# Opening a retention and convolution trunk layer pair by pair of channel tiles, with conditioning weights taken between the pairs

## The reference

```python
mod = silu(cond) @ ada_w + ada_b           # (…, 6*1024): sh1, sc1, g1, sh2, sc2, g2
sh1, sc1, g1, sh2, sc2, g2 = jnp.split(mod, 6, axis=-1)
h = rms_norm(x, n1_pre) * (1 + sc1) + sh1
proj = h @ w_in                            # q, k, v, g, u_a, u_b, two gates
```

## Time and profile before

| | us |
|---|---|
| median of 3 runs | 2121.06 (2118.7 to 2122.29) |
| the profiled execution | 2119.73 |
| its span | 2117.9 |

### The profile page before, as it was taken

How to read it: one execution, slowest core, us unless ns; L and a number is a source line. 1 busy time by engine, 2 the same in 40 slices (tenths; PEclk the granted TensorE clock), 3 DMA queues, 4 the chain that set the end, 5 groups by cost and what they waited for, 6 DMA issues and landing times.

```text
span 2117.9 us, 30759 instructions
## 1 busy us (share of the span) xinstructions
PE 2075.9 (98%) x12055; PEld 1876.0 (89%) x12055; DVE 1647.5 (78%) x1946; ACT 828.2 (39%) x1378; POOL 832.8 (39%) x557
## 2 busy tenths in 40 slices
PE   7999999999999999999999999999999999999998
PEld 3888887887887999999999998899999999978886
DVE  3599699699699587787536536699989989878867
ACT  3512212212212366565548323353433334344344
POOL 1414315315316366665381220006666565570000
PEclk9999999999999999999999999999999999999999
DMA  9343432432432455545464444312223223258453
GB/s 308 122 133 101 138 115 101 138 117 99 136 105 96 166 162 168 181 143 158 166 221 152 130 167 147 110 32 77 79 63 94 63 70 87 83 197 290 139 179 115
DMA packets 233760, 283.08 MB, mean 134 GB/s; under 512 B 11441, under 2 KB 176145, under 8 KB 233617
## 3 DMA queue, kind: packets, MB, share of 16 engines
q1 hardware_dynamic: 180785, 212.41, 31.7%
q10 hardware_dynamic: 51424, 63.98, 8.9%
q0 software_dynamic: 1408, 4.72, 0.6%
HBM read 214.06 MB, written 67.01 MB: 133 GB/s over the span
## 4 chain that ended last, share of the span: by engine, by line
PE 86%; DVE 5%; POOL 2%; ACT 2%; SPq 2%; DMA 1%; issue 1%; ACTq 0%; DVEq 0%; POOLq 0%
PE ps L1130 85%; DVE f_cv L2937 1%; PE ps L1345 1%; POOL Wa_lo L2288 1%; SPq L766 1%; DMA x_all<-in_x_sample 1%; DVE T_lo L2918 1%; DMA r_raw<-rT_d 0%; DVE T_raw L2892 0%; PE ps L1393 0%; PE ps L1480 0%; POOL ada_l L2288 0%; DMA W_raw<-in_w_in 0%; PE ps L1184 0%; DVE Al L2976 0%
## 5 line engine op out<-in xcount | busy, mean ns | idle before, releaser
L2590 DVE SCALAR_TENSOR_TENSOR conv_y<-u_in,VC,conv_y 128x1167 f32<-128x1167 f32 x240 | 409.1, 1704 | 11.1 <-ACT conv_y L1759 4.7
L1130 PE MATMUL ps<-A_hi,Wa_hi 128*128 128x384 f32 x768 | 261.1, 340 | 0.5 <-DVE A_lo L2538 0.5
L1130 PE MATMUL ps<-A_hi,Wa_lo 128*128 128x384 f32 x768 | 258.3, 336 | 0.0
L1130 PE MATMUL ps<-A_lo,Wa_hi 128*128 128x384 f32 x768 | 258.3, 336 | 0.0
L2438 POOL TENSOR_TENSOR O_lo<-E,O_hi 128x512 fp32r<-128x512 f32 x78 | 124.4, 1595 | 290.5 <-ACT O_hi L1637 290.5
L2937 DVE SCALAR_TENSOR_TENSOR f_cv<-f_in,VF,f_cv 128x1023 f32<-128x1023 f32 (+1 forms) x176 | 209.8, 1243 | 2.4 <-ACT f_cv L2105 0.6
L2288 POOL TENSOR_TENSOR Wa_lo<-W_raw,Wa_hi 128x1024 fp32r<-128x1024 f32 x51 | 133.6, 2627 | 195.6 <-ACT Wa_hi L1637 195.4
L2288 POOL TENSOR_TENSOR ada_l<-ada_w,ada_h 128x1024 fp32r<-128x1024 f32 x32 | 90.7, 2834 | 240.2 <-ACT ada_h L1637 240.1
L1130 PE MATMUL ps<-Wb_hi,A_lo 128*128 128x512 f32 x432 | 169.3, 392 | 0.0
L1130 PE MATMUL ps<-Wb_hi,A_hi 128*128 128x512 f32 x432 | 169.1, 391 | 0.0
L1130 PE MATMUL ps<-Wb_lo,A_hi 128*128 128x512 f32 x432 | 168.8, 391 | 0.0
(11 more groups left out here) (342 smaller groups left out, 5467.2 us busy)
## 6 DMA issues: line engine op xcount, KB each, us to landing
F_raw<-in_ffn_w_up SPq DMA_DIRECT2D x44, 512.0 KB, 6.1
qt<-qkvg_d SPq DMA_DIRECT2D x36, 512.0 KB, 3.6
W_raw<-in_w_in SPq DMA_DIRECT2D x32, 512.0 KB, 5.3
W_raw<-in_w_in SPq DMA_DIRECT2D x64, 256.0 KB, 3.3
ada_w<-in_ada_w ACTq DMA_DIRECT2D x30, 512.0 KB, 4.5
F_raw<-in_ffn_w_down SPq DMA_DIRECT2D x30, 512.0 KB, 4.8
A_raw<-g_d SPq DMA_DIRECT2D x25, 512.0 KB, 4.2
g_d<-f_cv SPq DMA_DIRECT2D x22, 576.0 KB, 3.6
```

The costliest lines, as they stand in the source:

```text
L1130: return pe.matmul(out, l, r, start=start, stop=stop)
L2590: dve.scalar_tensor_tensor(out=y, in0=x, scalar=tap, in1=y, op0=ALU.mult, op1=ALU.add).then_inc(q.conv_step, 1)
```

## The change

The opening is reordered, and nothing of what is computed changes. The eight pieces of `ada_w` become four **pairs**: pair `p` is the scale piece and the shift piece of channel tiles 2p and 2p+1. Each pair has its own product, row copy, turn and `hscale`. The steps are in the order `STEPS`: channel tiles 0 to 3 of group 0, then of group 1 (pairs 0 and 1), tiles 4 and 5 of both groups (pair 2), 6 and 7 of both (pair 3), and then all eight of the third group. `first_u` does both products of a step one after the other; the products of pairs 1 to 3 stand behind steps 1, 3 and 7, their turns behind 1, 4 and 8.

Banks are short, since six are filled by both products from the start: one bank (`MOD_BANK`) holds conditioning, and one (`TURN_BANK`) all turned blocks, so `x_turn(j)` waits until ACT has read the block before (`hT_f`). `modulated` writes into one of three SBUF buffers (`h_buf`) instead of PSUM, `halves` reads them there, and ACT no longer writes `A_hi`. The twelve parameter rows are issued by ACT, the exponentials of the decay tables stand behind the first weight splits, and the masks in DVE's step 4.

The diff, cut to its core:

```diff
-        TURN_BANK = (5, 7, 6)
-        ON_ACT = lambda j: j < 2 * KT and j % KT % 3 == 1
+        TURN_BANK, MOD_BANK, ROW_BANK = 6, 7, 3
+        STEPS = ([(g, k) for g in (0, 1) for k in range(4)] + [(g, k) for p in (2, 3) for g in (0, 1) for k in (2 * p, 2 * p + 1)]
+                 + [(2, k) for k in range(KT)])
+        PAIR_FROM = (0, 2, 8, 12)
+        ADA_BEHIND = {1: 1, 3: 2, 7: 3}
+        ADA_TURN_BEHIND = {4: 2, 8: 3}
+        h_buf = [sq_t[:, 1, 0:TG], sq_t[:, 1, TG:2 * TG], rows[:, 0:3, :].rearrange("p r n -> p (r n)")]
...
             chunk_load(0)
-            ada_chunk(7)
+            chunk_load(1)
+            ada_pair(0)
+            ada_pair(1)
             x_load(1)
-            chunk_load(1)
+            ada_pair(2)
+            ada_pair(3)
...
             def x_turn(j):
-                g, k = divmod(j, KT)
-                if j >= 3:
-                    pe.wait_ge(q.hT_lo, j - 2)
+                g, k = step_of(j)
+                if j:
+                    pe.wait_ge(q.hT_f, j)
+                pe.wait_ge(q.xn_ok, 3 * g + 3)
...
+            ada_early(0)
+            row_turns()
+            ada_turn(0)
...
+                for j in range(N_A):
+                    while turned < min(j + 3, 3 if j < 2 else 4 if j < 4 else 16 if j < 16 else N_A):
+                        x_turn(turned)
+                        turned += 1
+                    if j < N_A - 2:
+                        for e in range(2):
+                            product(e, j)
+                    if j in ADA_BEHIND:
+                        ada_early(ADA_BEHIND[j])
+                        if j == 1:
+                            ada_turn(1)
+                    if j in ADA_TURN_BEHIND:
+                        ada_turn(ADA_TURN_BEHIND[j])
+                for e in range(2):
+                    for j in (N_A - 2, N_A - 1):
+                        last = product(e, j)
+                    last.then_inc(q.u_ps, 1)
...
             squares(0)
             split_w(0)
-            squares(1)
-            act.wait_ge(q.mod_ok, 2)
+            split_w(1)
+            decay_exp()
             for j in range(N_A):
+                if j in PAIR_FROM:
+                    act.wait_ge(q.mod_ok, PAIR_FROM.index(j) + 1)
                 modulated(j)
-                if j == 7:
-                    squares(2)
-                if j in (3, 15, 19, 21, 23):
-                    split_w((3, 15, 19, 21, 23).index(j) + 1)
+                if j == 3:
+                    squares(1)
+                if 12 <= j < 15:
+                    square(j - 6)
+                if j == 15:
+                    root(2)
+                if j in (17, 19, 21, 23):
+                    split_w((17, 19, 21, 23).index(j) + 2)
...
             for j in range(N_A):
+                if j in (0, 2):
+                    ada_rows_out(j // 2)
+                if j in PAIR_FROM:
+                    mods(PAIR_FROM.index(j))
+                if j == 4:
+                    decay_masks()
+                if j in (4, 16):
+                    meaned(1 if j == 4 else 2)
+                    normed(1 if j == 4 else 2)
                 halves(j)
+                if j in ADA_TURN_BEHIND:
+                    ada_rows_out(ADA_TURN_BEHIND[j])
```

More of the change, by code:

```diff
@@ new lines, in _, with product @@
+            ada_early(0)
+            row_turns()
+            ada_turn(0)
+            def first_u():
+                turned = 0
+                pe.wait_ge(q.vec_ok, 6)
+                def product(e, j):
+                    g, k = step_of(j)
+                    tiles = slice(3 * g, 3 * g + 3)
+                    o = ps[:, 3 * e + g, 0:TG].rearrange("p (t n) -> p t n", n=P)
+                    wh, wl = (x[chunk_slot(e)].rearrange("p (k n) -> p k n", k=KT) for x in (w_hi, w_lo))
+                    pe.wait_ge(q.hT_lo, j + 1)
+                    mm(o, wh[:, k, :], A_hi[:, tiles, k, :], k == 0, False)
+                    mm(o, wh[:, k, :], A_lo[:, tiles, k, :], False, False)
+                    return mm(o, wl[:, k, :], A_hi[:, tiles, k, :], False, k == KT - 1)
+                for j in range(N_A):
[4 more added lines that the diff above has]
+                        for e in range(2):
+                            if j == 0:
+                                pe.wait_ge(q.w_lo, e + 1)
+                            product(e, j)
[9 more added lines that the diff above has]
+                    last.then_inc(q.u_ps, 1)
@@ L1409, in _ @@
                 if s == -5:
[L1410 removed]
+                    pe.wait_ge(q.mod_ok, 6)
                     pe.transpose(ps[0:64, 6, 0:P], gm1[:, :], ident[:, :]).then_inc(q.gain, 1)
@@ L2561, in _, with ada_rows_out, mods @@
-            for j in range(N_A):
-                if j == 3:
-                    normed(1)
-                if j == 8:
-                    meaned(2)
-                    normed(2)
+            decay_tables()
+            def ada_rows_out(p):
+                dve.wait_ge(q.vecT, ada_summed(p))
+                dve.tensor_copy(ada_row(p), ps[0:2, MOD_BANK, :].rearrange("c (v n) -> c v n", v=2)).then_inc(q.vec_ok, 1)
+            def mods(p):
+                dve.wait_ge(q.ada_used, 4 * (p + 1))
+                dve.wait_ge(q.vec_ok, 2)
+                two = slice(2 * p, 2 * p + 2)
+                for v in (SH1, SC1):
+                    r = v * KT + 2 * p
+                    c = 4 * v
+                    ins = dve.tensor_tensor(mod[:, r:r + 2, :], ps[:, MOD_BANK, c:c + 4].rearrange("p (k c) -> p k c", c=2),
+                                            col2(V_ADAB + r, 2), ALU.add)
+                then(ins)
+                dve.scalar_tensor_tensor(out=hscale[:, two, :], in0=mod[:, SC1 * KT + 2 * p:SC1 * KT + 2 * p + 2, :], scalar=1.0,
+                                         in1=col2(V_N1PRE + 2 * p, 2), op0=ALU.add, op1=ALU.mult).then_inc(q.mod_ok, 1)
```

225 lines of the change are left out of this document (89 added, 136 removed).

## The result

The changed kernel takes **2147.78 us** (median of 4 runs, 2145.52 to 2149.06), the kernel before 2121.07 on the same chip: a ratio of **1.0123, 95% interval 1.0112 to 1.0135**, 26.7 us slower. The forecast was 2143, range 2134 to 2152.

The account below looks back on a forecast made before the run. PE was taken as the bound: 85.4 of work + 14.4 waits + 5.0 port + 1.7 clock end `first_u` at 106.5. The later start made 2117.9 + 22 a span of 2140, median 2143 us, range 2134 to 2152.

Parts of the forecast that it names:

- Start: Opening: pair 0's product from 16.6 for 8.9 us, then an unhidden chain; first `first_u` product at 33.4 instead of 47.95.
- The central argument: After the first product: conditioning only moved on in-order PE; 52.0 us remain, ending at 85.4, so at best 1.5 us won.
- Waits and port: In `first_u`: PE's waits made by the pairs, 14.4 us, plus DVE's sums held by POOL's splits, 5.0.
- hand-over of pair 1: Behind pair 1's product: row copy, `hscale`, `modulated(2)`, turn and halves make PE wait 3.5 us.
- The port: Last steps of `first_u`: DVE's two-SBUF-input sums wait for POOL's split subtractions, 5.0 us (bounds 0 and 9.6).
- chain to `ada_l`: Behind the last halves: transfers, splits and `ada_l` up to the product, 22.2 us as before; what follows starts 22.7 later.
- Clock: Opening: only the hole before the first product drops PE's clock, twelve products mostly at 0.32; 1.7 us, bounds 0 and 6.
- a wait of 2 to 3 us for `ada_l`: Sign in the new trace: PE waits this long for `ada_l` in the fourth tile of `q_half(0)`.
- The waits close: Rival for `first_u`: halves and turns keep ahead, clock stays up, PE ends at 85.4; 2119 to 2123 us, chance 0.06.
- half of them close: Rival for `first_u`: port costs nothing, clock stays, DVE's SBUF instructions are quicker; loss 4.2 to 13 us, chance 0.08.
- More half clock: Rival for the opening: each hole lowers the clock and the last group runs at 0.32; 2153 to 2165 us, chance 0.06.
- It comes back later: Rival for everything after the opening: later slack gives the loss back; no share of its own.

Follow-up runs that it names:

- after_short: The changed kernel with only one of eight matmuls in each conditioning product of pairs 1 to 3; 2134.90 us, ratio 1.0067 to the kernel before.
- fill: The changed kernel plus 92 idle transposes on PE in places where it waits; 2146.63 us, ratio 1.0114 to the kernel before.
- fill_early: fill with the transfers of chunks 6 and 7 issued ahead of SP's wait for the last halves; 2140.69 us, ratio 1.0090 to the kernel before.
- splits: The changed kernel with the splits of weight chunks 2 to 5 moved beside pair 2's conditioning product; 2147.45 us, ratio 1.0118 to the kernel before.
- tuned_fill: The kernel before with group 1's normalising spread, chunk 1's split later, chunks 6 and 7 issued earlier, 32 idle PE transposes; 2119.94 us, ratio 0.9995.
- banks: The changed kernel with turned blocks in three banks again, two for the third group; 2146.25 us, ratio 1.0110 to the kernel before.
- squares: The changed kernel with the third group's squares, root and normalising moved to step 9, beside pair 3's product; 2148.26 us, ratio 1.0125.
- after_swap: The changed kernel with the conditioning product's operands exchanged (weight block stationary, two condition columns moving), no row copy or turns; 2166.04 us, ratio 1.0216.

## Why the prediction was right, point by point

**Start.** The pair's product at 17.57 and 9.14 long (forecast 16.6, 8.9), its end 26.7 (25.5), first product 34.07 (33.4). The chain that nothing hides went as written: ACT's exponentials 28.86 to 31.31, the first block behind them, then a round of 1.60 (31.92 to 33.52) and the last turns.

**The central argument held, its number was 2 too low.** Three conditioning products of about 7 us stand between products, and nothing hides them (after_short). But the work behind the first product is some 54 us, not 52.0. The 0.1735 a product was read where no turn stands between. A step with its turn is 1.38 us at full clock and not 1.29, since the first product behind the turn takes 0.26 (the changed kernel, PE's timeline):

```profile
66.23 0.42 PE L1133 MATMUL ps<-A_hi,Wa_hi 128*128 128x384 f32 x1
66.49 0.34 PE L1133 MATMUL ps<-A_lo,Wa_hi 128*128 128x384 f32 x1
...
67.37 0.49 PE L1183 MATMUL ps<-ident,x_all 128*128 128x128 f32 x3
67.61 0.42 PE L1133 MATMUL ps<-A_hi,Wa_hi 128*128 128x384 f32 x1
```

The earlier trace rows have it too (79.48 with 0.42). Some 24 such steps make 2 us, and a pair takes 7.0 and not 6.9. With 54 us from 34.07 on, PE would end at 88 if it never waited: not even the 1.5 us were to be won.

**Waits and port, 19.4, right as a sum.** In fill and fill_early, without any half clock, q - first is 73.3. Less 54 that is some 19.3, for the 14.4 + 5.0 of the sum. By PE's timeline of fill_early the hand-over of pair 1 is 3.1 (forecast 3.5), step 4 2.2 (2.0), steps 7 and 11 0.8 each (1.0, 0.9), the third group 4.2 (4.3), the last eight steps with port and last halves 7.2 (6.6). The port alone is less sure. In the changed kernel it lengthened `A_lo` by 4.5 us, but PE waited 2.9 for it, and taking it away gave 3.1 (splits), not 5.0; with the clock up the waits were 4.5 (fill_early). The Trainium skill's rule (SBUF — State Buffer, Who interferes with whom) held for the sums and for the normalising (2.55 us in tuned_fill where it takes 0.74 alone). What the sum did not see is that its terms aren't independent: one bank, ACT's pace and the port cover each other in the same eight steps. With the chain to `ada_l` that is why each edit alone gave half or less at the end.

**Clock, 1.7: the mis-sized term.** It is 6.3 net (79.65 less 73.32), just over the upper bound of 6. The step that failed is "I take the first alone": the clock fell five times, behind the first turns, pair 1's hand-over, the turns of step 4, those of the third group, and in the last two steps.

**From there to the end.** q was forecast at 106.5 and came at 113.7: 0.7 from the start, 4.6 from the clock, 1.9 from the work of PE. The last halves came at 110.65 (104.8), the chain behind them took 21.0 (22.2), so what follows starts 27.4 later, not 22.7. The sum itself then goes on with 22 where it had worked out 22.7; with that it would have said 2143.7, and the miss is 4.1 and not 4.8. The sign "a wait of 2 to 3 us for `ada_l`" didn't come: it was 0.60. The last halves lay 3.1 us before the end of `first_u`, not 1.65, since the last nine products ran at half clock (3.04 us), and the chain was 1.2 shorter. The chain is a term of its own, as the sum had it: banks, squares, splits and fill all lost part of their gain at `ada_l`.

**Rivals.** "The waits close" and "half of them close" fell with 11.9 us of idle PE in the stretch. "More half clock" had the mechanism right and the size too high: a mean of 0.86 over 79.65 us is some 22 us at 1.2 GHz, but only 6.3 of the 11 that this could cost show. A part of it lay where PE waited anyway (the hand-over of pair 1 takes 3.58 at either clock), and a part is what the port takes back at full clock. "It comes back later" had nothing for it: "rest" is 2031.0 and 2031.4.

## What to carry to other kernels

Splitting work that all goes through one in-order engine so that dependent work can start earlier wins only that engine's idle time. Here that was 1.5 us by the forecast's count and none by the pitch measured, and every cut added a hand-over through three engines, each with its wait and the longer ones with half clock behind them. Before moving steps, count what is left for the bounding engine from the new start on; if it fills the stretch, the early start is not a gain. And after speeding up a stage, look at the next chain that starts from it: here two transfers issued some 20 us earlier decided whether the 6 us won in the opening reached the end.

## What the runs showed that I had not expected

- A float32 product of a full 128x128 stationary block with two moving columns leaves two records of 0.112 us each at 2.4 GHz and 0.213 at 1.2 (after_swap); with two stationary columns and 256 moving it was 0.219 a record at 2.4. A transpose of a 128x128 block took 0.083.
- The granted clock fell from 1.00 to 0.50 in the middle of a product while PE was never idle (after_swap, about 88 us), so a hole is not the only thing that it falls behind.
- The moment at which the first pair's weights have landed varied from 17.29 to 19.66 us between kernels whose queues are the same up to there. `first` comes 15.2 to 17.2 us behind it, so it carries over into `first`; that it goes into the time was not tested by itself.
- The issue of the three rope transfers on SP took 1.45 to 1.60 us in most runs and 3.4 to 4.2 in others (3.83 in the kernel before). What decides it is open.
- "Rest" varied by more than the wait for `ada_l`. In several runs a stretch of some 4 us at 1.2 GHz follows a wait at a later stage boundary, in others it doesn't. In squares two stretches of 100 us (700 to 800 and 1000 to 1100) show 0.98 where the changed kernel and the kernel before have 1.00; all three show 0.98 from 1900 to 2000. By the mean clock each such stretch is worth about 2 us, an estimate. So 1 to 3 us between two kernels can come from places that the edit doesn't touch; what makes such a dip come or stay away was not tested.
